# Held weight parts behind tile 0, rests ahead of the norm, and sums on GpSimd in a three-block network

## The reference, cut to what matters

```python
def ada_modulation(c, ada_w, ada_b):
    m = jax.nn.silu(c) @ ada_w + ada_b          # 1024 -> 6 x 1024
    return jnp.split(m, N_MOD, axis=-1)         # shift, scale, gate (mixer); shift, scale, gate (feed-forward)

def even_layer(...):                            # odd_layer has the same frame around its attention
    h = modulate(rms_norm_2(x, mix_norm), sh_m, sc_m)
    ...                                         # mixer
    x = x + g_m[:, None, :] * y                 # y = mixer output @ w_out
    hf = modulate(rms_norm_2(x, ffn_norm), sh_f, sc_f)
    return x + g_f[:, None, :] * swiglu(hf, ffn_w_gate, ffn_w_up, ffn_w_down)

def swiglu(h, w_gate, w_up, w_down):
    return (jax.nn.silu(h @ w_gate) * (h @ w_up)) @ w_down
```

## Time and profile before

| what | value |
|---|---|
| median of three runs | 892.11 us |
| profiled execution, its span | 891.4 us, 889.3 us |
| TensorE busy | 880.2 us (99%) |
| VectorE busy | 694.1 us (78%) |
| ScalarE busy | 501.6 us (56%) |
| GpSimd busy | 29.0 us (3%) |
| TensorE clock granted | full throughout |

### The profile page before, as it was taken

One profiled execution on the slowest core, in us unless ns is written; L12 is line 12 of the kernel. 1 busy time (PEld: TensorE's weight loads), 2 busy tenths in 40 slices (PEclk: granted clock), 3 DMA queues, 4 the chain that ended last, 5 costly groups with the idle time before them and its releaser, 6 DMA issues.

```text
span 889.3 us, 13261 instructions
## 1 busy us (share of the span) xinstructions
PE 880.2 (99%) x4833; PEld 747.9 (84%) x4833; DVE 694.1 (78%) x735; ACT 501.6 (56%) x673; POOL 29.0 (3%) x52
## 2 busy tenths in 40 slices
PE   8999999999999999999999999999999999999998
PEld 5998878888888799979888888878777888888886
DVE  4698977988888987896888888687797875655655
ACT  5545665565555658756554455465675565545542
POOL 4000110000000100002000000010000000000000
PEclk9999999999999999999999999999999999999999
DMA  6989585899899384565988887536434366556551
GB/s 215 338 270 341 183 302 183 319 364 369 328 332 340 129 284 145 175 202 183 364 310 316 321 313 281 195 114 211 135 118 142 118 208 195 190 189 188 189 192 67
DMA packets 117091, 208.04 MB, mean 234 GB/s; under 512 B 7236, under 2 KB 81068, under 8 KB 111928
## 3 DMA queue, kind: packets, MB, share of 16 engines
q1 hardware_dynamic: 116566, 205.31, 67.1%
q10 hardware_dynamic: 290, 2.10, 0.7%
q0 software_dynamic: 192, 0.05, 0.0%
HBM read 206.39 MB, written 1.05 MB: 233 GB/s over the span
## 4 chain that ended last, share of the span: by engine, by line
PE 93%; DVE 4%; DMA 2%; issue 1%; ACT 1%; SPq 0%; DVEq 0%; ACTq 0%
PE ub L1937 11%; PE tp L1937 10%; PE acc L1837 7%; PE acc L1838 7%; PE acc L1840 7%; PE ub L1939 5%; PE acc L1800 5%; PE tp L1939 5%; PE acc L1802 5%; PE acc L1801 5%; PE tp L1957 4%; PE acc L1957 3%; PE acc L1923 3%; PE acc L1925 3%; PE acc L1924 3%; PE ub L2183 1%
## 5 line engine op out<-in xcount | busy, mean ns | idle before, releaser
L1157 DVE TENSOR_TENSOR w_lo<-w_raw,w_hi 128x1024 fp32r<-128x1024 f32 x283 | 341.8, 1222 | 105.1 <-ACT w_hi L728 104.7
L728 ACT ACTIVATE w_hi<-w_raw 128x1024 fp32r<-128x1024 f32 x283 | 296.8, 1057 | 211.9 <-PE acc L1840 49.8
L1937 PE MATMUL tp<-aT,w_hi 128*128 128x512 f32 x432 | 135.9, 396 | 0.0
L1937 PE MATMUL ub<-aT,w_hi 128*128 128x512 f32 x432 | 135.4, 395 | 0.0
L1837 PE MATMUL acc<-w_hi,hT_hi 128*128 128x512 f32 x284 | 110.8, 390 | 0.8 <-DVE w_lo L1157 0.8
L1838 PE MATMUL acc<-w_lo,hT_hi 128*128 128x512 f32 x284 | 110.6, 389 | 0.0
L1840 PE MATMUL acc<-w_hi,hT_lo 128*128 128x512 f32 x272 | 105.8, 389 | 0.0
L1939 PEld LDWEIGHTS tp<-aT,w_lo 128*128 128x128 f32 x432 | 81.2, 188 | 19.2
L1939 PEld LDWEIGHTS ub<-aT,w_lo 128*128 128x128 f32 x432 | 81.1, 188 | 18.9
L1939 PE MATMUL tp<-aT,w_lo 128*128 128x256 f32 x432 | 84.9, 278 | 0.0
L1939 PE MATMUL ub<-aT,w_lo 128*128 128x256 f32 x432 | 84.9, 278 | 0.0
(11 more groups left out here) (324 smaller groups left out, 1307.9 us busy)
## 6 DMA issues: line engine op xcount, KB each, us to landing
ada_raw<-in_l_ada_w SPq DMA_DIRECT2D x24, 1024.0 KB, 6.7
w_raw<-in_l_ffn_w_gate SPq DMA_DIRECT2D x44, 512.0 KB, 4.7
w_raw<-in_l_ffn_w_up SPq DMA_DIRECT2D x44, 512.0 KB, 3.8
w_raw<-in_l_ffn_w_down SPq DMA_DIRECT2D x44, 512.0 KB, 3.4
w_raw<-in_w_up SPq DMA_DIRECT2D x32, 512.0 KB, 4.8
w_raw<-in_w_down SPq DMA_DIRECT2D x32, 512.0 KB, 5.4
scratch<-in_l_ada_w SPq DMA_DIRECT2D x14, 1024.0 KB, 7.4
w_raw<-in_attn_w_qkv SPq DMA_DIRECT2D x24, 512.0 KB, 6.3
```

Of the source, the lines that this page charges most:

```text
L728: act.activation(rounded_part(v), w_raw[:, v % SLOTS, :], ACT.Copy).then_inc(hi_done, 1)
L1157: dve.tensor_tensor(rest_part(v), w_raw[:, v % SLOTS, :], rounded_part(v).bitcast(F32), ALU.subtract).then_inc(lo_done, 1)
L1937: pe.matmul(banks[f], rounded_part(v)[:, c[f]], aT[:, :, b, :], start=b == 0, stop=False)
```

## The change

- In A, B and C, the last four weight parts of the projection go to a new home, `hold`, which lies in `scratch` behind its first 2048 columns. Their rounding waits for what used that memory (`home_free`), not for a slot.
- In A and C, `out_last` does all of tile 0 first and then tile 1 of all four parts (before: tile 1 of part 0 first, of three parts behind). In B, `down_last` does tile 1 of three parts behind tile 0 and in halves.
- The four slots are free earlier, so all four parts of the next stage are rounded and their rests made ahead of the norm (before: one or two ahead of it, the others in its course).
- The norms of A, B and C go by halves on ScalarE, with a third GpSimd instruction per tile; `entry_ahead` has another order of products, in which all parts are released at the end.
- Ten of layer 2's twelve sums are taken from TensorE and done by GpSimd's `partition_all_reduce`, 512 columns each: four once the accumulation of the first third is there, four when the second third is, two behind norm 5. The row blocks of `ada_w` come third by third for that. Two sums stay on TensorE in B.

```diff
 # homes
-            (U_WOUT0 + 2, (aT_hi[:, 4:KB, :], aT_lo[:, 4:KB, :])),
-            (U_QKV2 - 1, (aT_hi[:, 4:KB, :], aT_lo[:, 4:KB, :])),
-            (U_WOUT1 + 2, (aT_hi[:, 0:4, :], aT_lo[:, 0:4, :])))}
+            (U_WIN - 2, (aT_hi[:, 4:KB, :], aT_lo[:, 4:KB, :])))}
+        held = {2 * u + n: homes[n] for u, homes in ((U_WOUT0 + 2, (3, 2, 1, 0)), (U_QKV2 - 2, (3, 2, 0, 1)),
+                                                     (U_WOUT1 + 2, (0, 1, 3, 2))) for n in range(4)}
+        apart.update({v: (hold[:, 2 * n, :], hold[:, 2 * n + 1, :]) for v, n in held.items()})
 # step table of layer 1's mixer (H: parts rounded, L: rests, U: TensorE unit)
-    U11 H13 L13 I0 U12 H14 U13""")
+    U11 H13 L13 I0 H14 L14 U12 H15 L15 U13""")
 # GpSimd
+            def rstd_halves():
+                for t in range(NT):
+                    ...
+                    pool.wait_ge(sq_half, n_half[0])
+                    chained(pool.tensor_scalar(var[:, t:t + 1], half_sums[:, 2 * t:2 * t + 1], EPS, None, ALU.add))
+                    pool.wait_ge(sq_done, n_rstd[0])
+                    chained(pool.tensor_tensor(var[:, t:t + 1], half_sums[:, 2 * t + 1:2 * t + 2], var[:, t:t + 1], ALU.add))
+                    pool.tensor_tensor(rstd[:, t:t + 1], var[:, t:t + 1], half[:, 0:1], ALU.pow).then_inc(rstd_done, 1)
+            def partition_sums(src, c0, c1):
+                for n in range(c0, c1):
+                    pool.partition_all_reduce(mod[:, n * CH:(n + 1) * CH], src[:, (n - c0) * CH:(n - c0 + 1) * CH], P,
+                                              bass.bass_isa.ReduceOp.add).then_inc(pool_sum, 1)
...
-            row_rstd()
+            pool.wait_ge(ada_used, 24)
+            partition_sums(mod_next, 0, 4)
+            pool.wait_ge(ada_used, 32)
+            partition_sums(mod[:, UNIT:2 * UNIT], 4, 8)
+            rstd_halves()
...
+            pool.wait_ge(xn_done, 24)
+            partition_sums(GATE_F, 10, 12)
 # VectorE, all three boundaries
+            def gated_norm(n, first, half, u_end, g_mod, g, shift):
+                dve.wait_ge(*first)
+                gated(0, g_mod, 0).then_inc(x_half, 1)
+                dve.wait_ge(tile0_done, n + 1)
+                gated(0, g_mod, 1).then_inc(x_ready, 1)
+                dve.wait_ge(x_ready, 2 * n + 1)
+                norm_scale(0, g)
+                norm_rows(0, g, shift)
+                dve.wait_ge(*half)
+                gated(1, g_mod, 0).then_inc(x_half, 1)
+                dve.wait_ge(w_used, parts_to(u_end))
+                gated(1, g_mod, 1).then_inc(x_ready, 1)
+                norm_lo(0, 0)
+                norm_lo(0, 1)
+                dve.wait_ge(x_ready, 2 * n + 2)
+                norm_scale(1, g)
+                norm_rows(1, g, shift)
+                norm_lo(1, 0)
+                norm_lo(1, 1)
 # VectorE, last slice of layer 1's feed-forward
+                def final(v, j):
+                    ...
+                    split_part(2 * v + 5)
+                    split_part(2 * v + 6)
+                    split_part(2 * v + 7)
+                    if not layer:
+                        split_part(2 * v + 8)
+                    ...                         # u_sum, h_ready
+                    if not layer:
+                        split_part(2 * v + 9)
+                    hidden_lo(j)
+                    if not layer:
+                        split_part(2 * v + 10)
+                        split_part(2 * v + 11)
...
+                    ada_gain(1, 1, pool_sum, 4)
 # TensorE
+            def entry_ahead(u, banks, behind_T0=None, out_before_T1=0, gated=False):
+                ...
+                norm_T(k, 0)
+                if behind_T0:
+                    behind_T0()
+                for p in order:
+                    pe.wait_ge(n_hi, 4 * k + 1 + group(p))
+                    part_ready(2 * u + p)
+                    products(0, p, aT_hi, rounded_part, begin=p == 0)
+                    products(0, p, aT_hi, rest_part)
+                for n, p in enumerate(order):
+                    if n == 2:
+                        ...
+                        norm_T(k, 1)
+                    pe.wait_ge(n_lo, 4 * k + 1 + group(p))
+                    products(0, p, aT_lo, rounded_part, end=p == 3)
+                for p in order:
+                    pe.wait_ge(n_hi, 4 * k + 3 + group(p))
+                    products(1, p, aT_hi, rounded_part, begin=p == 0)
+                    products(1, p, aT_hi, rest_part)
+                for p in range(4):
+                    pe.wait_ge(n_lo, 4 * k + 3 + group(p))
+                    products(1, p, aT_lo, rounded_part, end=p == 3).then_inc(w_used, 1)
```

More of the change, by code:

```diff
@@ L142, in block_program @@
         qk_gain = sb("qk_gain", [P, 2])
+        with nc.sbuf_tensor("below_hold", [P, UNIT], F32), nc.sbuf_tensor("hold", [P, 8, PART], F32R) as hold:
+            pass
         scratch = sb("scratch", [P, 10240])
@@ L604, in swiglu @@
                     sp.wait_ge(x_ready, 6)
-                with sp.Fori(0, (NJ_SG - 3) // 2) as i:
-                    for q in range(2):
-                        one(2 + q, i, q if layer == 0 else None)
+                for third in range(2):
+                    with sp.Fori(0, (NJ_SG - 3) // 4) as i:
+                        for q in range(2):
+                            one(2 + 4 * third + q, i, 1 + third if layer == 0 else None)
                 one(NJ_SG - 1)
@@ L1950, in products @@
                 def products(t, p, op, w, begin=False, end=False):
-                    v, blocks = 2 * u + p, 4 if gated else 2
-                    part = w(v)
-                    for n in range(blocks):
-                        b = 4 * (p % 2) + n if gated else 2 * p + n
-                        out = banks[t][:, HALF * (p // 2):HALF * (p // 2 + 1)] if gated else banks[t]
-                        width = HALF if gated else CH
-                        last = pe.matmul(out, op[:, b, t * P:(t + 1) * P], part[:, n * width:(n + 1) * width],
-                                         start=begin and n == 0, stop=end and n == blocks - 1)
-                    return last
-                def half(t, p):
-                    pe.wait_ge(n_hi, 4 * k + 2 * t + 1 + (p % 2 if gated else p // 2))
+                    part = w(2 * u + p)
+                    for n in range(2):
+                        last = pe.matmul(banks[t], op[:, 2 * p + n, t * P:(t + 1) * P], part[:, n * CH:(n + 1) * CH],
+                                         start=begin and n == 0, stop=end and n == 1)
+                    return last
                 norm_T(k, 0)
@@ L2023, in out_unit, with out_last @@
                         lo_count=lo_count, parts=parts)
-            def out_last(u, order, lo_count=0, sums=()):
+            def out_last(u, order, ahead=None):
                 v, h = 2 * u + 4, order[2][1]
@@ L2059, in out_last @@
                 last.then_inc(tile0_done, 1)
-                if sums:
-                    ada_sums(1, *sums)
-                for p in (1, 2, 3):
+                for p in range(0 if ahead else 1, 4):
                     tile(1, p).then_inc(w_used, 1)
```

376 lines of the change are left out of this document (175 added, 201 removed).

## The result

The changed kernel takes 911.26 us (median of 6 runs, 909.15 to 916.16) against 891.35 us: 1.023 times as long (95% interval 1.0218 to 1.0246), 19.9 us more. I had forecast 897.3, with a range from 889.5 to 908. The direction was right and the size was not. The profiled execution took 910.66 us.

The account below looks back on a forecast made before the run. TensorE's list laid end to end was taken as the bound. Boundaries A, B, C added 4.2 + 0.3 + 0.7 = 5.2 us, removed sums included, to 891.4: 896.6 profiled, 897.3 median; range 889.5 to 908, own range 893.4 to 901.

Parts of the forecast that it names:

- A: Boundary from layer 1's attention (`w_out`) to its feed-forward: end at 413.0 against 408.84, +4.2 us; +2.2 with early gate, free add.
- B and C: Boundaries into layer 2's `w_qkv` (B, +0.3 us) and from layer 2's attention to its feed-forward (C, +0.7 us).
- all of it on the path: Layer 2's sums taken from TensorE at A, B and C: 7.8 us, all on the path that sets the end.
- T0: Tile 0's transposes on TensorE at each boundary; forecast at 397.6 for A, 582.0 for B, 698.8 for C.
- Nobody waits: GpSimd's partition sums, about 7 us each: done well before their users at 560 us and behind, so no wait.
- between 0 and 1 us: Cost of the partition sums through what they do to VectorE's rests, reading in short pieces.
- the wait at the exit: End of each entry: slots released late, so the loop's first product waits 0.85 us more for a rest.
- The 5.6 us from the gate to T0: At A: two gated halves 2.75 us, 2.1 until rows can start, 0.75 for their first half.
- T1: Tile 1's transposes, the second ones; at A TensorE reaches them after 6.25 us, then 0.45 us of waiting.
- up to 1.5: At B: a load of w_qkv that lands late would add up to 1.5 us.
- Rival 1: A partition sum holds VectorE's rests in layer 1's feed-forward: at 3 us each, 18 us more, 915; chance 0.14.
- Rivals 2 and 3: At A, B, C: 2, gaps covered and removed work won, 886.9 us (0.12); 3, a wash, 892 to 893.9 (0.13).

Follow-up runs that it names:

- run 6: Kernel before, with layer 2's sums on TensorE cut to two of their 512 columns, waits and copies kept: 890.49 us, ratio 0.9992.
- Runs 1 to 3: In order: changed kernel, ten partition sums replaced by one-column memsets, 903.96 us; kernel before plus one last partition sum, 896.95; changed kernel, identity by VectorE, 904.41.
- run 5: Changed kernel with VectorE's gates of tile 0 put back ahead of three of the four rests at A, B and C: 906.77 us, ratio 1.018.
- run 8: Changed kernel with tile 1's last products reordered at A, B and C so the first part's slot is released earlier: 907.08 us, ratio 1.017.
- run 4: Changed kernel with extra matmuls nobody reads filling TensorE's gaps ahead of the norms' transposes, six at A, two each at B and C: 907.47 us.
- run 1: Changed kernel with each of GpSimd's ten partition sums replaced by a memset of one column: 903.96 us, ratio 1.014.
- Run 9: Changed kernel with identity by VectorE, earlier slot release, tile 0's gates ahead of all rests, squares ahead of last roundings, earlier gain at A: 900.89 us.

## Why the prediction was right and wrong

**What bounds the kernel.** I wrote that "an instruction taken from that list is worth its full time". That sentence failed. The rows of the kernel before had shown TensorE's list without gaps; run 6 shows that its sums stood where it would otherwise have waited for VectorE and ScalarE. The 7.8 us "all of it on the path" were worth about 0.7 us there. In the sum this did less harm than it might, since I had placed T0 at each boundary by VectorE's chain from the gate; the misses are in what follows.

**The start: the largest miss, 5.2 us.** The step that failed is the term of the partition sums. I had written "Nobody waits" and put them at "between 0 and 1 us"; TensorE waits 5.9 us for GpSimd's constants at the start; I had looked only at the users of the sums, at 560 us and behind. No step, rival or bound had it. Without it the time would have been about 906, inside the range, and still 9 us above the forecast. I had bounded the partition sum by its own duration (0.9 to 58 us) and by what it does to VectorE, not by what its presence does to GpSimd's first instructions. Runs 1 to 3 show the cost, that the instruction's presence brings it, and that TensorE's wait for the identity is how it counts.

**A: 6.0 for 4.2.** T0 lies 3.9 us later than before, counted from the start of A, as forecast (397.6 against 393.69). Shown right: the rests ahead of the gate (run 5), the loads that make the last two late, the wait at the exit (1.0 to 1.2 us for 0.85; run 8). The 5.6 us from the gate to T0 (5.63 measured) came out with a little luck. GpSimd's add ended at 401.24, right behind `norm_scale` (401.19), as I had let it, but after 0.40 us and not 1.2, since it began only when ScalarE's sum was read; the 0.25 us that I had put behind it weren't there, and handovers of about as much that I had not counted were. On the way to T1 the power took 1.59 us, in `norm_scale`'s time. What was missing is that TensorE's rate doesn't stay: 1.5 us at the granted clock of 0.5 (run 4).

**B and C: 4.0 and 2.6 for 0.3 and 0.7.** The gates came 1.2 us (B) and 1.3 us (C) later than my chains of rests had them. At B the rounding of the last parts waited for their loads (1.2 us idle on ScalarE), the risk that I had put at "up to 1.5" beside the forecast and not in it. At C the last part's load was 1.2 us later than I had it, and the gap was 2.3 us for 1.7. No run moved the loads by themselves; their share is read from the waits. Behind T0, B lost 1.5 us by the clock. T1 to the end cost 0.4 to 0.7 us more than my count at each of A, B and C.

**The partition sums.** 3.2 to 4.1 us for my 7; nobody waited for a result. Rival 1's mechanism is real: 1.5 us of hold each on VectorE, as a mean. Of the 12.2 us in layer 1's feed-forward 11 were hidden in its idle time. I had set the point from which it decides at 1 us of hold; at 1.5 the ten cost 1.4 us in all (run 1). The likely reason is that the rests' lead refills between the holds; no run tests that.

**Rivals 2 and 3** needed gaps that are covered. Run 9 covered T0's at A and C (1.2 us remain at B) and showed that this isn't enough: the next thing late is T1. A wash wasn't near.

**The sum of the misses:** 5.2 (start) + 1.8 (A) + 3.7 (B) + 1.9 (C) + 1.7 (both feed-forwards; my "0 to 1" was in the range and not in the sum) = 14.3 us in the span, of which 0.3 come off outside it, for the 14.0 us between 897.3 and 911.3. My own range for the sum ended at 901 (its terms give 891.4 + 8.2 + 0.7 = 900.3) and the whole at 908, because each of its bounds came from a term of the sum, and the largest cost was in no term.

No version that I ran beats the kernel before and computes the same. Left open: what GpSimd does in its waits, 10 to 12 us ahead of the first select or iota and 6.0 us ahead of 421.78 and of 728.52. That they come with the instruction's presence is shown; nobody was behind the later ones. The Trainium skill's "GPSIMD Engine Reference", section 2.1, "Instruction dispatch", tells of kernels that are loaded into GpSimd at run time, and that the first call to a freshly loaded one pays about 6 us which no instruction in the profile shows. The later waits agree with it; the first one, 10.1 to 12.0 us, is longer than the page says, and it falls on a select or iota that the kernel before has too. I had not weighed that page; by its figure alone the wait would have stood ahead of the sums, where it costs nothing.

## What to carry to other kernels

An engine at 99% may be full because fillers stand in its waits; before counting removed work, look at what would be ready at that moment on the engines that feed it, and count the list of that engine between the two events instead. An instruction of a new kind is bounded by its duration, by what it holds, and also by what its presence in the program does to others; a run with one of it, placed where it can't matter, measures that for itself. A gap on TensorE costs its length and can bring a stretch at the lower granted clock behind it: 1.5 us at A and at B here, nothing at C.

## What the runs showed of the hardware

- With one `partition_all_reduce` in the program GpSimd stood still for 10.1 to 12.0 us ahead of its first select or iota, and for 5.7 to 6.2 us ahead of a later group of partition sums that follows other work. All eight kernels with such an instruction show it, none of the five without.
- A partition sum of 128x512 f32 takes 3.2 to 4.3 us over all runs, one of 128x128 1.09 us, and a VectorE subtraction of 1.22 us beside it up to 3.4 us. The Trainium skill's "SBUF — State Buffer", section "Who interferes with whom", speaks of exclusion for a whole instruction. Here it was less: a subtraction that began at 428.88, inside the sum of 428.17 to 431.48, ended at 431.57 after 2.69 us, where 1.22 us behind the sum's end would be 432.7. So the sum excludes VectorE only in parts of its run.
- Behind TensorE gaps of 5.1 to 5.5 us at A the granted clock was 0.5 for 6.8 us in all four profiled executions that had one. Behind gaps of 1.4 to 3.0 us it was 0.5 for 3.4 or 6.8 us in some and 1.0 in others, also for the same length: 2.25 us at B brought 3.4 us, 2.31 us at C nothing. With the gaps filled it stayed at 1.0 in all four executions.
- The 128x512 products whose weights lie in `hold` start 0.233 us apart, and those of the same parts before 0.227 us. That is 0.9 us for the 144 of them; in the changed kernel it lies ahead of TensorE's gaps and costs nothing. Why they are slower is open.
